# Hybrid DeltaNet/attention backbone on one core: layer 1's modulation products from the grouped attention to the DeltaNet part

## The reference, cut to what matters

```python
for layer in range(DEPTH):                                  # DEPTH = 2, D_MODEL = 1024, F32
    mod_l = split((silu(c) @ ada_w[layer] + ada_b[layer]), 6)         # latents
    mod_c = split((silu(c_ctx) @ ada_w[layer] + ada_b[layer]), 6)     # context
    a_lat, a_ctx = modulate(h, ln1, mod_l[0], mod_l[1]), modulate(hc, ln1, mod_c[0], mod_c[1])
    if layer % 2 == 0:    # projection; DeltaNet heads AND grouped attention (GQA); one output projection
        y_lat, y_ctx = even_mixer(a_lat, a_ctx, ...)
    else:                 # neighbourhood attention
        y_lat = odd_mixer(a_lat, a_ctx, ...)
    h = h + mod_l[2] * y_lat
    h = h + mod_l[5] * expert_choice_ffn(modulate(h, ln2, mod_l[3], mod_l[4]), ...)   # 16 experts
    ...                   # the same for the context hc in layer 0
return rms_norm(h, final_norm_g)
```

## Time and profile before

| | |
|---|---|
| time, median of 3 runs | 2298.76 us (2296.31 to 2300.56) |
| profiled execution, time | 2309.88 us |
| its span, first to last instruction | 2308.1 us |
| PE busy | 2101.9 us (91%) |
| DVE busy | 746.7 us (32%) |
| ACT busy | 495.5 us (21%) |
| POOL busy | 163.6 us (7%) |
| mean granted TensorE clock | 0.950 |

### The profile page before, as it was taken

One profiled execution on the slowest core, in us unless ns is written; L12 is line 12 of the kernel. 1 busy time (PEld: TensorE's weight loads), 2 busy tenths in 40 slices (PEclk: granted clock), 3 DMA queues, 4 the chain that ended last, 5 costly groups with the idle time before them and its releaser, 6 DMA issues.

```text
span 2308.1 us, 33045 instructions
## 1 busy us (share of the span) xinstructions
PE 2101.9 (91%) x13898; PEld 1068.7 (46%) x13898; DVE 746.7 (32%) x1402; ACT 495.5 (21%) x1167; POOL 163.6 (7%) x139
## 2 busy tenths in 40 slices
PE   6998999838799799999999989999999599999997
PEld 3544666537784333333333334554774244444442
DVE  3243526597763510111010132000772411111113
ACT  2213456545551110000000011000551100000001
POOL 0000015301110001110011000000000000000000
PEclk9999999957589899999999999999999799999999
DMA  7229766432144389999999972110214599999996
GB/s 289 74 78 347 252 208 206 172 147 105 44 157 164 144 312 367 386 387 395 385 388 388 402 281 71 55 37 30 94 34 193 203 401 420 421 421 420 420 420 271
DMA packets 120302, 576.25 MB, mean 250 GB/s; under 512 B 14000, under 2 KB 26800, under 8 KB 72672
## 3 DMA queue, kind: packets, MB, share of 16 engines
q1 hardware_dynamic: 112048, 546.67, 60.3%
q0 software_dynamic: 7168, 23.83, 3.6%
q10 hardware_dynamic: 944, 3.67, 0.4%
HBM read 537.59 MB, written 34.96 MB: 248 GB/s over the span
## 4 chain that ended last, share of the span: by engine, by line
PE 78%; DMA 10%; DVE 8%; issue 2%; ACT 2%; SPq 0%; DVEq 0%; POOLq 0%; ACTq 0%
PE ps L2436 24%; PE ps L2448 5%; PE ps L550 5%; PE ps L1927 4%; DMA ring_sb<-expert_w_up 4%; PE ps L978 4%; PE ps L2805 3%; DMA work_sb<-expert_w_up 3%; PE ps L1968 2%; PE ps L2777 2%; PE ps L2786 2%; PE ps L2466 2%; PE ps L2486 2%; PE ps L977 2%; PE ps L246 2%
## 5 line engine op out<-in xcount | busy, mean ns | idle before, releaser
L2436 PE MATMUL ps<-work_sb 128*32 128x512 f32 (+1 forms) x2416 | 423.2, 594 | 8.2 <-DMA work_sb<-expert_w_up 5.5
L2436 PE MATMUL ps<-ring_sb,work_sb 128*32 128x512 f32 (+1 forms) x1984 | 287.8, 604 | 18.8 <-DMA ring_sb<-expert_w_up 12.2
L2436 PEld LDWEIGHTS ps<-work_sb 128*32 128x32 f32 (+1 forms) x2416 | 128.4, 120 | 218.2 <-issue 215.4
L2436 PEld LDWEIGHTS ps<-ring_sb,work_sb 128*32 128x32 f32 (+1 forms) x1984 | 82.3, 117 | 197.4 <-issue 188.1
L2627 DVE TENSOR_TENSOR work_sb<-ps,work_sb 128x512 f32<-128x512 f32 x32 | 20.6, 686 | 443.6 <-PE ps L2448 338.6
L2558 ACT ACTIVATE work_sb<-ps 128x1024 f32<-128x1024 f32 x16 | 16.4, 1023 | 512.6 <-PE ps L2448 293.8
L550 PE MATMUL ps<-ring_sb,work_sb 128*128 128x512 f32 (+1 forms) x288 | 108.1, 537 | 1.7 <-ACT work_sb L518 1.7
L2568 ACT COPY work_sb<-ps 128x512 f32<-128x512 f32 x32 | 17.3, 588 | 414.2 <-PE ps L2524 414.1
L2448 PE MATMUL ps<-ring_sb,work_sb 128*32 128x512 f32 x768 | 102.0, 601 | 0.0
L2448 PE MATMUL ps<-work_sb 128*32 128x512 f32 x768 | 100.7, 592 | 0.0
L978 PE MATMUL ps<-work_sb,ring_sb 128*128 128x512 f32 x192 | 98.1, 592 | 0.0
(11 more groups left out here) (442 smaller groups left out, 3027.8 us busy)
## 6 DMA issues: line engine op xcount, KB each, us to landing
work_sb<-expert_w_down SPq DMA_DIRECT2D x70, 1024.0 KB, 18.0
work_sb<-expert_w_gate SPq DMA_DIRECT2D x68, 1024.0 KB, 12.1
work_sb<-expert_w_up SPq DMA_DIRECT2D x68, 1024.0 KB, 14.9
ring_sb<-expert_w_gate SPq DMA_DIRECT2D x52, 1024.0 KB, 8.9
ring_sb<-expert_w_up SPq DMA_DIRECT2D x50, 1024.0 KB, 16.4
ring_sb<-expert_w_down SPq DMA_DIRECT2D x50, 1024.0 KB, 14.5
ring_sb<-ada_w SPq DMA_DIRECT2D x96, 512.0 KB, 6.1
ring_sb<-wout SPq DMA_DIRECT2D x16, 512.0 KB, 6.4
```

The source lines that it names most:

```text
L2436: mm = pe.matmul(ps[g:g + wide, bank + n, :], lat_src[:, k, g:g + wide], us[e][:, n * 512:(n + 1) * 512], start=(k == 0), stop=(k == KT - 1))
```

## The change

It does four things. (1) Of layer 1's 48 units, 16 stay in the grouped attention, one pair in every other step; 32 leave it, the ring and SP's list. (2) The 32 become "late" units: POOL loads them into three slots in the upper half of `H`, PE multiplies 16 of them in `prep_pe` of group 1, between the two Gram tiles, and 16 in `levels_pe` of group 1, between its stages, into bank 2; DVE adds the bias after inverse 0 and after the 27 steps of inverse 2. (3) So that `H` is free, SP writes the six grouped outputs to DRAM (`grouped_rows`) ahead of the decay loads, and reads them back from there at the end. (4) Five semaphores become one counter, `gates_d`, with the same order of events.

```diff
+        def late_unit(n):
+            return H[:, 2 * (n % 3):2 * (n % 3) + 2, 512:1024]
+        def late_matmuls(pe, n, bank):
+            _, r, k, i = ada_unit(1, n)
+            pe.wait_ge(ada_land[(n - 16) % 3], 16 * ((n - 16) // 3 + 1))
+            w = late_unit(n - 16)
+            for a in range(2):
+                q = 2 * (n % 2) + a
+                mm = pe.matmul(ps[32 * q:32 * q + 32, bank, :], sT[:, k, :], w[:, a, :], start=(k == 0), stop=(k == KT - 1))
+            mm.then_inc(ada_mm, 1)
+        def late_units(pool, lo, hi):
+            for n in range(lo, hi):
+                if n >= 19:
+                    pool.wait_ge(ada_mm, n - 18)
+                pool.dma_start(late_unit(n - 16), ada_unit(1, n)[0].rearrange("p (a n) -> p a n", a=2)) \
+                    .then_inc(ada_land[(n - 16) % 3], 16)
...
-        for count in (1, 2, 1, 2, 2, 1, 2, 1, 2, 2, 1, 1, 2, 1, 2, 1):
-            MODULATION.append([(1, m) for m in range(done, done + count)])
+        MODULATION += [[(1, n // 2)] if n % 2 == 0 else [] for n in range(16)]
...  prep_pe, in front of the second Gram tile
+                if (g, t_) == (1, 1):
+                    for n in range(16, 32):
+                        late_matmuls(pe, n, 2)
+                    pe.wait_ge(rows_ok, 5)
...  levels_pe: after stage 1; after each tile of stage 2; after each of stage 3; after stage 4
+            def modulation(first, count):
+                if g == 1:
+                    if first == 0:
+                        pe.wait_ge(dn_rm, muls(2, 3))
+                    for n in range(32 + first, 32 + first + count):
+                        late_matmuls(pe, n, 2)
+            modulation(0, 3)
+                modulation(3 + 2 * t_, 2)
+                modulation(7 + 2 * t_, 2)
+            modulation(11, 5)
+            if g == 1:
+                pe.wait_ge(rows_ok, 6)
...  dn_dve
             inverse.end()
+            ada_rows_dve(dve, 1, 1, 2)
...
                 inverse.steps(24 if g == 0 else 27)
+                if g == 1:
+                    ada_rows_dve(dve, 1, 2, 2)
                 chunks_dve(dve, g, step, inverse, 1)
...  decays_first
+            for tt in range(NT):
+                sp.dma_start(grouped_rows[tt], YC[:, tt, 512:1024]).then_inc(rows_in, 16)
```

More of the change, by code:

```diff
@@ L248, in ada_matmuls @@
             mm.then_inc(w_free, 1)
+        ada_mm = sem("ada_mm")
+        ada_land = [sem(f"ada_land{i}") for i in range(3)]
+        def late_unit(n):
[14 more added lines that the diff above has]
+                    .then_inc(ada_land[(n - 16) % 3], 16)
         def finish_bank(l, r):
@@ L277, in ada_gates_pe @@
                     pe.wait_ge(gq_o, NT)
-                    pe.wait_ge(rows_ok, 6)
+                    pe.wait_ge(rows_ok, 4)
                 for a in range(2):
@@ L295, in ada_rows_dve @@
             row = GROW if (l, r) == (0, 2) else ROWS[:, r, :]
-            dve.wait_ge(w_free, ada_at(l, 16 * r + 15) + 1)
+            if l == 1 and r > 0:
+                dve.wait_ge(ada_mm, 16 * r)
+            else:
+                dve.wait_ge(w_free, ada_at(l, 16 * r + 15) + 1)
             nc.vector.tensor_tensor(row, ps[:, bank, :], row, ALU.add).then_inc(rows_ok, 1)
@@ L470, in build @@
         U_ADA[1] = len(stream)
-        for n in range(48):
+        for n in range(16):
             add("ada", 1, n)
@@ L480, in build @@
         tp_mm, tp_dve, tp_act = sem("tp_mm"), sem("tp_dve"), sem("tp_act")
-        ab_x, ab_e, ab_la, ab_beta = sem("ab_x"), sem("ab_e"), sem("ab_la"), sem("ab_beta")
-        g_mm, g_act, g_diff, g_rowT, g_rows = (sem(n) for n in ("g_mm", "g_act", "g_diff", "g_rowT", "g_rows"))
+        gates_d, ab_e = sem("gates_d"), sem("ab_e")
+        g_mm, g_act, g_rows = (sem(n) for n in ("g_mm", "g_act", "g_rows"))
         bqk_ok, bqt_mm, bqt_dve, bqt_act = (sem(n) for n in ("bqk_ok", "bqt_mm", "bqt_dve", "bqt_act"))
@@ L602, in gates_logs_dve @@
                                     bc(DTB.rearrange("p (d h) -> p d h", d=2).unsqueeze(1), [P, NT, 2, 8]),
-                                    ALU.add).then_inc(ab_x, 1)
+                                    ALU.add).then_inc(gates_d, 1)
             dve.wait_ge(ab_e, 5)
@@ L639, in gates_sums_pe @@
         def gates_sums_pe(pe):
-            pe.wait_ge(ab_la, 1)
+            pe.wait_ge(gates_d, 2)
             pe.wait_ge(masks_in, 16)
@@ L650, in gates_rows_pe @@
         def gates_rows_pe(pe):
-            pe.wait_ge(ab_beta, 1)
-            pe.wait_ge(g_diff, 1)
+            pe.wait_ge(gates_d, 3)
+            pe.wait_ge(gates_d, 4)
             for tt in range(NT):
@@ L730, in build @@
         MODULATION = [[(0, 8 + 2 * n), (0, 9 + 2 * n)] for n in range(8)]
-        done = 0
-        for count in (1, 2, 1, 2, 2, 1, 2, 1, 2, 2, 1, 1, 2, 1, 2, 1):
-            MODULATION.append([(1, m) for m in range(done, done + count)])
-            done += count
-        ROWS_AT = (4, 8, 13, 18)
+        MODULATION += [[(1, n // 2)] if n % 2 == 0 else [] for n in range(16)]
+        ROWS_AT = (4, 8)
         SCORES = ps[:, 0:3, :].rearrange("p b n -> p (b n)")
@@ L742, in gqa_pe @@
             pe.wait_ge(g_act, 1)
-            pe.wait_ge(g_rowT, 1)
+            pe.wait_ge(gates_d, 5)
             def scores(n):
@@ L1736, in dn_pool @@
             zero_pool(0)
+            pool.wait_ge(rows_in, 16 * (3 + NT))
+            late_units(pool, 16, 32)
             eye_pool(pool, 1)
@@ L1740, in dn_pool @@
                 keys_pool(pool, i)
+            late_units(pool, 32, 35)
             eye_pool(pool, 2)
             levels_pool(pool, 1)
+            late_units(pool, 35, 48)
             keys_pool(pool, 4)
```

24 lines of the change are left out of this document (12 added, 12 removed).

## The result

| | median | lowest to highest | profiled span |
|---|---|---|---|
| before | 2299.66 us (4 runs) | 2296.31 to 2301.43 | 2308.1 us |
| after | 2315.57 us (4 runs) | 2311.47 to 2317.22 | 2313.7 us |

The ratio is 1.0062, with 95% between 1.0043 and 1.0082: the change costs 14.3 us (10 to 19), over the 0.2% that count as a difference. The forecast was 2304.5 us (+5.7). The measured time lies 11 us above it, 1.4 us inside the upper end of the range (2317 us); what came is the size of rival D (+15 us, 2314 us). So I compare places up to those levels.

The account below looks back on a forecast made before the run. PE was taken to bound the grouped attention, DVE's chain the DeltaNet part, where PE idles. Terms -10.3 + 4.8 + 11.2 = +5.7 us on the median 2298.8 gave 2304.5 us, range 2293 to 2317 us.

Parts of the forecast that it names:

- rival D: Both bursts: single matmuls after waits take 1.94 us, a turn 6.3 us; sum +15 us, 2314 us; chance 0.23.
- The gain of the grouped attention: Latent steps of the grouped attention: fewer modulation pairs on PE shorten them, until the score loop limits; -10.3 us.
- What costs nothing: SP's six output writes delay decay loads to 323.4 us, before ACT asks at 325.35; end reads and merged counter also free.
- Burst 1: Units 16 to 31 in `prep_pe` of group 1: five turns of 5.4 us make DVE's add wait; +4.8 us.
- the cover: Time hiding the first sixteen late units: from PE's start at 473.8 us to DVE's bias add at 498.9 us.
- Burst 2: Units 32 to 47 in `levels_pe` of group 1: DVE gets the chunk's first product at 612.6, not 601.4 us; +11.2 us.
- the walk: Stage-by-stage timing of units 32 to 47 among group 1's levels, with 4.1 us landings, done at 609.7 us.
- rival C: Levels of group 1 run at full clock because 512-column products keep PE active; -7.5 us, 2291 us; chance 0.12.
- B: Both bursts: turns of 4.8 us or less, landing at 3.5 us; -1.5 us, 2297 us; chance 0.23.
- The Trainium skill's rule: Late loads: 2.0 us plus bytes by 436 GB/s, 3.2 us for 512 KB; turn 4.5 us, sum -1.9 us, 2297 us.
- my own case: Both bursts: turns of 5.2 to 6.2 us; sum +5.7 us, 2304.5 us; chance 0.42.
- Queue against DVE: POOL's descriptors beside DVE's steps: two-input products should be harmless; if not, an estimated +2 us in each burst.

Follow-up runs that it names:

- e1: The change without units 16 to 47 of layer 1's modulation, their loads, products and adds; 2287.95 us, 0.9953 of before.
- e2: The change without units 32 to 47, their loads, products and add, leaving only the first sixteen late units; 2299.66 us, 1.0011 of before.
- e7: The change with filler products keeping PE busy between the late units 16 to 31; 2317.64 us, 1.0072 of before.
- run 0: Not a follow-up run: a stretch of chunks inside the kernel, from prep 1's first product to inverse 1's end; 70.5 us in e7, 64.7 in the change.
- e6: The change with five slots in place of three for units 16 to 31; 2305.83 us, 1.0019 of before.
- e8: The change with 32 units kept in the grouped attention, only sixteen late, through five slots, started earlier; 2294.02 us, 0.9974 of before.
- e10: e8 with its first five late units moved ahead of the second tile's transposes in prep 1; 2293.92 us, 0.998 of before.
- e5: e2 with its sixteen late loads issued by ACT on its own hardware queue; 2298.48 us, 0.9996 of before.
- e4: The change with only the first three late loads made, all products and adds kept, weights wrong; 2293.78 us, 0.9982 of before.

## Why the prediction was right or wrong, point by point

- **The gain of the grouped attention (-10.3): right**, 10.88 us by the trace and 10.8 by e1. The step without units is 5.29 us, where the one early step of before had said 5.40.
- **What costs nothing: right.** Timeline of ACT in after; the decay instruction (L1442) stands right behind the convolution's copy, without a wait:

```profile
312.35 0.59 ACT L1022 COPY work_sb<-ps 128x512 f32<-128x512 f32 x1
312.83 4.79 ACT L1442 ACTIVATE work_sb<-work_sb 128x128 f32<-128x128 f32 x16
```

- **Burst 1 (+4.8): the term was too small, it measured +10.9**, by the trace, and +11.7 by e2 less e1. Start and end of the cover were right: from PE's first unit to DVE's readiness 25.1 us forecast, 24.6 measured (462.55 to 487.18). The step that failed is "a turn is 4.1 + 1.07 + 0.25 = 5.4 us". It was 6.55. Of the 1.15 us missing, 0.64 are landing (4.74 for 4.1) and the other 0.5 PE's use with its semaphores (1.81 for 1.32). Five turns make 5.7 us and the cold last unit 0.9. The sum had already added 1 us for full DMA engines, and the cover was 0.5 us shorter: 5.7 + 0.9 - 1.0 + 0.5 is the 6.1 us between forecast and trace. The cold value, 1.94 us, stood in a row of before; for 512 KB loads that follow each other on this queue there was no row. What was wrong was to read `fin_g`, one load by itself, as the price of three that follow each other, and "I take the warm one, since PE works right before": that held for the first three units. After the wait of 4.87 us the window of 470 to 475 us shows 0.50, and units 19 to 24 take 1.92 us each.
- **Burst 2 (+11.2): the term was too small, it measured +17.0, of which 2.9 came back.** The walk's order was right, with its end at the last landing and `rows_ok` in front of the chunk. The granted clock of 0.50 in stages 2 and 3 was right. The term that failed is the landing of 4.1 us: the load of unit 37, issued at 576.40 us next to two of SP's, in the stretch whose DMA share reaches 1.04, took 8.6 us, so that PE had the unit 2.7 us later than in the walk (22.5 us behind inverse 1's end for 19.7). By the end of the last unit the walk is 5.7 us short (50.9 for 45.2): the loads of 46 and 47 took 4.5 and 5.1 us, and the last unit 1.92 us and not 1.1. That a faster chunk would give something back I had only under rival C (3 us); 2.9 us came back without C.
- **The rivals.** B (turns of 4.8 us or less) is out by every run. The Trainium skill's rule, "DMA: Bandwidth & Descriptors", section "Anatomy of one DMA", with its estimate of 3.2 us, goes with it: the shortest landing of a late load in any run was 3.9 us. C is out by the 0.50 in the levels. D had the total (+15), the turn (6.3 for 6.55) and both bursts nearly right (by its own turn its burst 1 comes to 9.1 us and not to the 8.5 that I wrote, and to 10.1 with the 1 us for full engines). But its reason, cold products, is less than half of it: e7 took the cold products away and 9.42 us of wait were left. I had given D 0.23 and my own case 0.42; the rows bear D's price better, with the rest in the landings. That D's total fits so well is in part luck, since it left the longer landings out and had nothing coming back from the chunk.
- **Queue against DVE.** Landings are no longer beside DVE's steps than without them: 4.10 us for the load issued at 478.20 us, beside DVE's inverse, and 4.13 for the one at 487.54 us, when DVE waited, both some 4 us behind the load before. Every issue on POOL took 0.72 to 0.78 us in the change, with and without them. With that the Trainium skill, "SBUF — State Buffer", section "Who interferes with whom", is borne out where it calls two-input products harmless.

Open is how much of a following load's longer landing is its data queueing behind the one before and how much is else: the 1.25 us between two landings explain unit 31 (issued 0.80 us behind unit 30 and landed 1.26 behind it), but not that unit 30 itself took 5.2 us, with 2.3 us between its landing and the one before. Open is also what made the clock rise later in e7's run 0.

## What to carry to other kernels

Work moved to an idle engine is worth the gain where it was and costs what its supply needs where it goes: count the turns of the few slots against the time that covers them. There is one turn less than the deepest slot has uses, and each is landing, use and semaphores. Take the landing from loads that follow each other, not from one by itself, and the use at the clock that the engine has after waiting. And price the gain piece by piece: here the first 16 units out of the attention brought 6.9 us, the next 16 only 3.9, and moving just the first half, through five slots and behind the one cover that could hold it, turned 14 us lost into 6 won.

## What the runs showed of the hardware

- The landing of a late load (512 KB) in burst 1 depended more on what else was in flight than on the queue. In the change it took 4.1 to 4.4 us when the load before had been issued 2.3 us or more ahead and the next one followed by 1.2 us or more; 4.9 to 5.7 us when it was issued 0.8 to 1.9 us behind another; 5.4 to 6.5 us in the first round, three at once. Of the five of a second round issued at once it took 5.9 to 8.3 us in e6, 7.0 to 9.6 in e8 and 6.9 to 12.1 in e10. Beside SP's loads it took up to 8.6 us (change, burst 2) and 9.7 us (e5, on ACT's queue).
- Late loads in flight together landed 1.25 us apart or more, with one exception of 1.1 us in e7.
- ACT issues such a load in 374 ns (e5), POOL in 722 (the change), both medians.
- A modulation unit takes 1.05 us when awaited at full clock (e7) and 1.92 at half (the change), but 0.44 us each when sixteen stand in a row at full clock (e4, 7.07 us).
- A faster engine in a loop with the DMA queues gained almost nothing (e7): granted clock 1.00 in place of 0.66 in the mean from 465 to 497 us, the burst as long as before.
